# A decoder trunk's first norm: input turned unscaled and kept for the residual, the norm's factor multiplied in after the turn, the rounding split over ACT, DVE and POOL

## The reference

```python
xn = rms_norm(x, norm1_g)            # x * rsqrt(mean(x*x) + 1e-6) * g
z  = xn @ w_in + b_in                # 1024 x 7176: LRU input, q, k, v, o, gates i and f, merge gates A and B
ha = rg_lru(causal_dwconv(u), ...)   # branch A, a recurrence over positions
hb = mlstm_seq(q, k, v, i, f, ...)   # branch B, 4 heads, chunks of 64
merged = sigmoid(gA) * (ha @ w_branch_a) + sigmoid(gB) * (hb @ w_branch_b)
x = x + merged @ w_out               # the residual
x = x + ConvFFN(rms_norm(x, norm2_g))
y = rms_norm(x, final_g)
```

## Time and profile before

| | |
|---|---|
| time, median of 3 runs | 1083.74 us (1082.34 to 1083.84) |
| profiled execution | 1083.24 us, span 1081.4 us |
| PE busy | 1064.2 us, 98% |
| DVE, ACT, POOL busy | 600.7, 397.7, 367.1 us |
| DMA, mean | 101 GB/s, 109.39 MB |

### The profile page before, as it was taken

How to read it: one execution, slowest core, us unless ns; L and a number is a source line. 1 busy time by engine, 2 the same in 40 slices (tenths; PEclk the granted TensorE clock), 3 DMA queues, 4 the chain that set the end, 5 groups by cost and what they waited for, 6 DMA issues and landing times.

```text
span 1081.4 us, 19445 instructions
## 1 busy us (share of the span) xinstructions
PE 1064.2 (98%) x8029; PEld 1037.4 (96%) x8029; DVE 600.7 (56%) x946; ACT 397.7 (37%) x565; POOL 367.1 (34%) x174
## 2 busy tenths in 40 slices
PE   6999999999999999999999999999999999999997
PEld 5999999999999999899899999999999999999997
DVE  5776558845252252342543338999950189999412
ACT  6566786323433334232423343223221122222332
POOL 3343334333222222222223344433444244334330
PEclk9999999999999999999999999999999999999999
DMA  6333332236263362352462233223313222223312
GB/s 175 108 85 91 101 91 79 80 107 142 78 191 96 88 219 59 101 173 88 147 166 63 81 95 98 79 84 93 100 56 102 76 79 78 79 88 99 100 43 89
DMA packets 180689, 109.39 MB, mean 101 GB/s; under 512 B 7691, under 2 KB 176891, under 8 KB 180606
## 3 DMA queue, kind: packets, MB, share of 16 engines
q1 hardware_dynamic: 180396, 108.12, 34.7%
q10 hardware_dynamic: 210, 0.07, 0.0%
HBM read 93.56 MB, written 12.41 MB: 98 GB/s over the span
## 4 chain that ended last, share of the span: by engine, by line
PE 98%; DMA 1%; ACT 0%; DVE 0%; SPq 0%; issue 0%; DVEq 0%
PE ring L1922 48%; PE ring L2317 22%; PE bank L2317 17%; PE bank L2178 2%; PE bank L2165 1%; PE bank L1971 1%; PE bank L2148 1%; PE bank L2158 1%; PE bank L2218 1%; PE bank L2043 1%; DMA x_tok<-in_x_prompt 1%; PE bank L2206 1%; PE ring L2076 1%; PE bank L2241 0%; PE ring L1962 0%; PE bank L1950 0%
## 5 line engine op out<-in xcount | busy, mean ns | idle before, releaser
L837 POOL TENSOR_TENSOR wlo<-stage,whi 128x1024 fp32r<-128x1024 f32 x79 | 197.3, 2497 | 425.8 <-ACT whi L883 425.8
L1922 PE MATMUL ring<-xh,whi 128*128 128x282 f32 (+1 forms) x1008 | 223.7, 303 | 0.0
L1922 PE MATMUL ring<-xl,whi 128*128 128x282 f32 (+1 forms) x1008 | 218.0, 298 | 0.0
L1922 PE MATMUL ring<-xh,wlo 128*128 128x282 f32 (+1 forms) x1008 | 217.5, 297 | 0.0
L1922 PEld LDWEIGHTS ring<-xh,whi 128*128 128x128 f32 x1008 | 162.5, 188 | 8.0 <-issue 7.6
L870 POOL TENSOR_TENSOR wlo<-stage,whi 128x1024 fp32r<-128x1024 f32 (+1 forms) x40 | 109.3, 2733 | 162.9 <-ACT whi L1225 162.9
L1922 PEld LDWEIGHTS ring<-xl,whi 128*128 128x128 f32 x1008 | 163.7, 188 | 0.0
L1922 PEld LDWEIGHTS ring<-xh,wlo 128*128 128x128 f32 x1008 | 163.4, 188 | 0.0
L883 ACT ACTIVATE whi<-stage 128x1024 fp32r<-128x1024 f32 x80 | 84.3, 1054 | 87.9 <-PE ring L1922 81.4
L1225 ACT ACTIVATE whi<-stage 128x1024 fp32r<-128x1024 f32 (+1 forms) x40 | 46.0, 1154 | 100.4 <-PE ring L2317 54.0
L870 POOL TENSOR_TENSOR wlo_third<-stage,whi_third 128x1024 fp32r<-128x1024 f32 (+1 forms) x20 | 52.9, 2643 | 83.4 <-ACT whi_third L1225 83.4
(11 more groups left out here) (372 smaller groups left out, 2239.7 us busy)
## 6 DMA issues: line engine op xcount, KB each, us to landing
stage<-in_w_in SPq DMA_DIRECT2D x56, 512.0 KB, 3.8
stage<-in_w_up SPq DMA_DIRECT2D x44, 512.0 KB, 3.7
stage<-in_w_down SPq DMA_DIRECT2D x16, 704.0 KB, 4.6
stage<-in_w_branch_a SPq DMA_DIRECT2D x8, 512.0 KB, 3.9
c_sample<-in_state_mlstm_C SPq DMA_DIRECT2D x16, 256.0 KB, 5.1
out_s_mlstm_C<-c_sample SPq DMA_DIRECT2D x16, 256.0 KB, 2.4
stage<-in_w_branch_b SPq DMA_DIRECT2D x8, 512.0 KB, 4.0
stage<-in_w_out SPq DMA_DIRECT2D x8, 512.0 KB, 3.9
```

The source lines that it names most:

```text
L837: pool.tensor_tensor(wlo[:, slot, 0:n], stage[:, slot, 0:n], whi[:, slot, 0:n].bitcast(F32), ALU.subtract).then_inc(w_lo, 1)
L1922: last = pe.matmul(of(z, t0, t1), w[:, kk * P:kk * P + P], x[:, kk, t0:t1], start=kk == 0 and m == 0, stop=kk == kn - 1 and m == 2)
```

## The change

x is turned as it is loaded. ACT copies each turned job from the ring to `x_raw` (unscaled, in the place that merged takes later). The norm's factor becomes a row spread over all partitions: DVE multiplies the identity by the tile's factors (`diag`), PE multiplies a matrix of ones with it, ACT copies the result to `rrow`. DVE then multiplies ring, norm gain and rrow into one of four buffers `xn_full`, ACT rounds that to xh, POOL subtracts for xl. PE's steps wait for POOL (`xn_lo`). SP writes x_raw (2.42 MB) to a DRAM tensor `x_turned` in one DMA after the m state, ahead of weight 3, and reads it back into resid in one DMA where x_tok2 was loaded. The turns of x_tok2 and ACT's copies of them go. Tile 4's square moves to DVE, weight 1's low part from POOL to DVE, and POOL clears bd after the last difference.

```diff
@@ SP
-            load_x(x_tok, x_in)
+            for i in range(TT):
+                load_tile(x_tok, x_in, i)
...
                 sp.dma_start(mst, a["state_mlstm_m"][0].rearrange("b h -> h b")).then_inc(gate_rows_in, 16)
+
+            sp.wait_ge(raw_done, XN)
+            sp.dma_start(xdram, flat(x_raw[:, :, :])).then_inc(x_spill, 16)
...
-            load_x(x_tok2, [x2_in] * TT)
+            sp.wait_ge(hb_lo, 8)
+            sp.wait_ge(x_spill, 16)
+            sp.dma_start(flat(resid[:, :, :]), xdram).then_inc(x2_in, 16)
@@ POOL
+            def xn_low(n):
+                f, t0, t1 = job(n)
+                pool.wait_ge(xn_hi, n + 1)
+                pool.tensor_tensor(xl[:, f, t0:t1], xn_full[n % 4][:, 0:t1 - t0], xh[:, f, t0:t1].bitcast(F32),
+                                   ALU.subtract).then_inc(xn_lo, 1)
+            for n in range(4):
+                xn_low(n)
             pool.wait_ge(w_hi, 1)
             pool.tensor_tensor(gate_columns(glo), ...).then_inc(w_lo, 1)
-            lo(1, 1, D)
+            for n in range(4, XN):
+                xn_low(n)
             st.link(pool.memset(bd[0][:, :, :], 0.0))
             pool.memset(bd[1][:, :, :], 0.0).then_inc(bd_zero, 1)
+            pool.wait_ge(w_lo, 2)
             lo(2, 0, D)
@@ ACT
-            act.activation(x_tok[:, 0], x_tok[:, 0], ACT.Copy, scale=rms[:, 0:1]).then_inc(x0_scaled, 1)
...
+            def raw_copy(n):
+                act.wait_ge(tile_done, T_XN + n + 1)
+                act.activation(x_raw[:, f, t0:t1], ring_bank(n)[:, 0:t1 - t0], ACT.Copy).then_inc(raw_done, 1)
+            def row_copy(part):
+                act.wait_ge(rb_psum, part + 1)
+                act.activation(rrow[:, t0:t1], bank[:, 3 - part, 0:t1 - t0], ACT.Copy).then_inc(rb_ready, 1)
             def xn_high(n):
-                act.wait_ge(tile_done, T_XN + n + 1)
-                act.activation(xh[:, f, t0:t1], ring_bank(n)[:, 0:t1 - t0], ACT.Copy, scale=cols[...])
+                act.wait_ge(tile_evicted, T_XN + n + 1)
+                act.activation(xh[:, f, t0:t1], xn_full[n % 4][:, 0:t1 - t0], ACT.Copy).then_inc(xn_hi, 1)
...
+            for n in range(4):
+                raw_copy(n)
+            rms_of(1)
+            row_copy(0)
             square_tile(2)
             rms_of(2)
             for n in range(4):
                 xn_high(n)
+                raw_copy(n + 4)
+                if n == 1:
+                    rms_of(3)
...             (gate columns rounded)
             rms_of(4)
+            xn_high(4)
+            hi(1, 1, D, None, 16)
+            xn_high(5)
+            row_copy(1)
+            raw_copy(8)
+            raw_copy(9)
+            xn_high(6)
+            xn_high(7)
+            raw_copy(10)
+            raw_copy(11)
+            for n in range(8, 12):
                 xn_high(n)
+                raw_copy(n + 4)
+            for n in range(12, XN):
                 xn_high(n)
             hi(2, 0, D, None, loads_of(2))
...
-                    for e in range(2 if residual else 0):          # in wb_pair
-                        act.wait_ge(res_done, 2 * f - 8 + e + 1)
-                        act.activation(flat(resid[:, ds(2 * f - 8 + e, 1), :]), bank2(e)[:, 0:T], ACT.Copy)
@@ DVE
+            def rms_diag(i):
+                dve.wait_ge(rms_done, i + 1)
                 st.link(dve.reciprocal(rms[0:n, i:i + 1], rms[0:n, i:i + 1]))
-                ts(x_tok[0:n, i], x_tok[0:n, i], rms[0:n, i:i + 1], None, ALU.mult).then_inc(x_scaled, 1)
+                ts(diag[i][0:n, 0:n], ident[0:n, 0:n], rms[0:n, i:i + 1], None, ALU.mult).then_inc(diag_done, 1)
+            def xn_scaled(n):
+                dve.wait_ge(rb_ready, n // 8 + 1)
+                dve.wait_ge(raw_done, n + 1)
+                if n >= 4:
+                    dve.wait_ge(xn_lo, n - 3)
+                mul_add(xn_full[n % 4][:, 0:t1 - t0], ring_bank(n)[:, 0:t1 - t0], cols[:, C_N1 + f:C_N1 + f + 1],
+                        rrow[:, t0:t1], ALU.mult, ALU.mult).then_inc(tile_evicted, 1)
+            order: diag 0, square 1, diag 1, scaled 0-3, diag 2, squares 3 and 4, diag 3, scaled 4 5, diag 4,
+                   scaled 6 7, low part of weight 1, scaled 8-15
...
             dve.wait_ge(tile_evicted, T_OUT)
-            dve.wait_ge(res_evicted, 8)
+            dve.wait_ge(x2_in, 16)
@@ PE
-                    if i:
-                        pe.wait_ge(x_scaled, i)
-                    else:
-                        pe.wait_ge(x0_scaled, 1)
+                    pe.wait_ge(x_in[i], 32 if i in (0, TT - 1) else 16)
                     last = pe.transpose(ring_bank(n)[...], x_tok[0:m, i, P * f:P * f + P], ident[0:m, 0:m])
...
-                pe.wait_ge(tile_evicted, T_XN + 8 * part + kk + 1)     # part_step
+                pe.wait_ge(xn_lo, 8 * part + kk + 1)
...
+            def rms_rows(part):
+                for i in tiles:                                         # 0, 1 or 2, 3, 4
+                    pe.wait_ge(diag_done, i + 1)
+                    last = pe.matmul(bank[:, 3 - part, ...], ones[0:m, :], diag[i][0:m, 0:m], ...)
+                last.then_inc(rb_psum, 1)
+            rms_rows(0)
-            for n in (4, 6):
+            for n in range(4, 8):
                 next_turn(n, range(2))
-                next_turn(n + 1, range(2))
-                gate_step(0, n - 4)
-                gate_step(0, n - 3)
+            for kk in range(2):
+                gate_step(0, kk)
+            rms_rows(1)
+            for kk in range(2, 4):
+                gate_step(0, kk)
             for n in range(8, 12):
                 gate_step(0, n - 4)
                 next_turn(n, range(2, TT))
             for n in range(12, XN):
                 next_turn(n, range(2, TT))
                 gate_step(1, n - 12)
                 first_step(0, 2 * n - 24)
                 first_step(0, 2 * n - 23)
...
-                for e in range(2 if f >= 4 else 0):                     # after w_branch_b's columns
-                    n = 2 * f - 8 + e
-                    if n >= 2:
-                        pe.wait_ge(res_evicted, n - 1)
-                    token_transposes(bank2(e), n, x_tok2).then_inc(res_done, 1)
```

More of the change, by code:

```diff
@@ L285, in hybrid_layer @@
         resid = sb("resid", [P, 8, T], o_b)
+        x_raw = sb("x_raw", [P, 8, T], o_c)
+        diag = [sb(f"rms_diag{i}", [P, P], o_b + 8 * D + 512 * i) for i in range(TT)]
+        xn_full = [sb(f"xn_full{i}", [P, T - SPLIT], o_b + 8 * D + 512 * TT + 4 * (T - SPLIT) * i) for i in range(4)]
         x_tok = sb("x_tok", [P, TT, D], o_h)
+        rrow = sb("rms_row", [P, T], o_h + 4 * D * TT)
         SB = 6 * TB + 10272 + 384
+        assert 4 * D * TT + TB <= SB
         def head_slot(name, shape, off):
@@ L1192, in _, with wb_pair @@
             hi(B_WB + 1, (B_WB + 1) % 2, D, T_WB, loads_of(B_WB + 1))
-            def wb_pair(i, residual):
+            def wb_pair(i):
                 for j in range(2):
@@ L1354, in scale_tile @@
                 st.link(dve.reciprocal(rms[0:n, i:i + 1], rms[0:n, i:i + 1]))
-                ts(x_tok[0:n, i], x_tok[0:n, i], rms[0:n, i:i + 1], None, ALU.mult).then_inc(x_scaled, 1)
-            def xn_low(n):
+                ts(diag[i][0:n, 0:n], ident[0:n, 0:n], rms[0:n, i:i + 1], None, ALU.mult).then_inc(diag_done, 1)
+            def xn_scaled(n):
                 f, t0, t1 = job(n)
-                dve.wait_ge(xn_hi, n + 1)
-                mul_add(xl[:, f, t0:t1], ring_bank(n)[:, 0:t1 - t0], cols[:, C_N1 + f:C_N1 + f + 1],
-                        xh[:, f, t0:t1].bitcast(F32), ALU.mult, ALU.subtract).then_inc(tile_evicted, 1)
-            dve.wait_ge(rms_done, 1)
-            dve.reciprocal(rms[:, 0:1], rms[:, 0:1]).then_inc(x0_inv, 1)
-            square_tile(1)
-            scale_tile(1)
-            square_tile(3)
-            dve.wait_ge(tile_evicted, T_XN)
-            xn_low(0)
-            xn_low(1)
-            scale_tile(2)
-            xn_low(2)
-            xn_low(3)
-            scale_tile(3)
-            scale_tile(4)
-            for n in range(4, XN):
-                xn_low(n)
+                dve.wait_ge(rb_ready, n // 8 + 1)
[4 more added lines that the diff above has]
+                        rrow[:, t0:t1], ALU.mult, ALU.mult).then_inc(tile_evicted, 1)
+            dve.wait_ge(const_done, 2)
+            rms_diag(0)
+            square_tile(1, 0)
+            rms_diag(1)
+            dve.wait_ge(tile_evicted, T_XN)
+            for n in range(4):
+                xn_scaled(n)
+            rms_diag(2)
+            square_tile(3, 1)
+            square_tile(4, 2)
+            rms_diag(3)
+            xn_scaled(4)
+            xn_scaled(5)
+            rms_diag(4)
+            xn_scaled(6)
+            xn_scaled(7)
+            dve.wait_ge(w_hi, 2)
+            dve.wait_ge(w_lo, 1)
+            tt(wlo[:, 1, 0:D], stage[:, 1, 0:D], whi[:, 1, 0:D].bitcast(F32), ALU.subtract).then_inc(w_lo, 1)
+            for n in range(8, XN):
+                xn_scaled(n)
```

(15 more changed lines are left out.)

61 lines of the change are left out of this document (23 added, 38 removed).

## The result

The changed kernel takes 1100.37 us, median of 6 runs (1099.88 to 1103.05), against 1083.22 (1082.34 to 1083.84) for the kernel before: a ratio of 1.0165, 95% interval 1.0152 to 1.0178. The profiled execution is the slowest of the six: 1103.05 us with a span of 1101.3, against 1083.24 and 1081.4 before. PE is busy 1067.0 us (before 1064.2) and 97% of the span. It does forty transposes less and ten short matmuls more (the norm row's), so nearly all of the 20 us are waits and a slower pace.

What follows compares the result with a forecast made beforehand. The prediction took PE's queue plus its few gaps as the bound: 1083.24 (profiled) - 4.08 (second turn) + 18.5 (late product 2, front's 7 included) + 1.6 (clock) = 1099.2 us. Own range 1095 to 1105, with rivals 1090 to 1108.

Steps and rivals of the forecast that it cites:

- Second turn, -4.08: Branch-b stage: removing PE's four groups of x_tok2 turns, 1.02 us each, saves 4.08 us; nothing else comes late there.
- The loop, 1.8 us a job: Front, second part: turn, raw copy, rounding, difference and gate step wait in a circle, 1.8 us a job against 1.46.
- rival B: Front and spill: the loop never forms and the spill holds nothing, product 2 at 41.2, total 1080.6 us; chance 0.05.
- Product 1 at 40.3: End of the front: PE's product 1 starts at 40.3 us instead of 33.24, so the front alone is +7 us.
- the walk: Front: four queues stepped through in written order with estimated durations, PE changing to its faster pace at 18.5 us.
- rival C: Front: gaps keep PE at its 1.2 GHz level, product 2 at 66.0, total 1107 us; chance 0.10.
- bd's clearing and SP's queue: Behind the front: POOL's clearing ends at 37.9, SP reaches the spill at 43.2 and issues weight 3 at 43.6 us.
- The spill, weight 3 landing 11.4 us behind its issue: SP's queue: 2.42 MB ahead of weight 3 delay its landing to 54.6 us; product 2 starts at 58.3 instead of 39.8.
- Rival A: SP's queue: the spill does not hold weight 3, product 2 at 51.1, half the clock's charge, total 1091.3 us; chance 0.13.
- The clock, +1.6: PE after its 11 us gap before product 2: 3.3 us at half pace cost 1.6 us, bounds 0 to 1.7.
- Sum: Whole kernel: 1083.24 - 4.08 + 18.5 + 1.6 = 1099.2 us, the 18.5 containing the front's 7; forecast's chance 0.70.

Runs made afterwards that it cites:

- e4: Kernel before without the second turn: PE's forty transposes and ACT's copies out, resid loaded from w_up, residual not computed; 1079.64 us, ratio 0.9970.
- e7: e4 with ACT's wait for m_lo moved behind the rounding of w_out's second weight, residual not computed; 1078.28 us, ratio 0.9958 to the kernel before.
- e8: e6 with ACT's wait for m_lo moved behind the rounding of w_out's second weight, nothing left out; 1082.85 us, ratio 1.0000 to the kernel before.
- e5: e2 with turns 8 to 11 and 12 to 15 ahead of each part's gate steps in PE's queue; 1084.13 us, ratio 1.0011 to the kernel before.
- e1: Changed kernel with the spill cut to 32 bytes a partition, resid loaded from w_up, residual not computed; 1095.73 us, ratio 1.0118 to the kernel before.
- e2: Changed kernel with POOL clearing bd before the sixteen differences instead of after them; 1088.74 us, ratio 1.0057 to the kernel before.
- e3: Changed kernel with bd cleared first and the spill cut to 32 bytes a partition, residual not computed; 1089.41 us, ratio 1.0058 to the kernel before.
- e6: e5 with the gate columns rounded and subtracted behind job 1 instead of job 3; 1084.15 us, ratio 1.0011 to the kernel before.
- b4: Kernel before without second turn: xh and xl spilled, read back and summed by DVE, branch-b weights but the last rounded one step ahead; 1083.10 us, ratio 0.9998.
- b5: b4 with weights rounded ahead in the last branch-b column and w_out too, and DVE's sums begun earlier; 1083.06 us, ratio 1.0000 to the kernel before.

## Why the prediction was right

The forecast was 1099.2 us and the time is 1100.37; the mechanism is the one forecast. That it came within 1.2 us is partly luck. All three quantities that its own range rests on fell outside their bounds: bd was clear at 42.2 (36 to 40), the landing took 10.0 (10.9 to 14.9), the clock cost 2.43 (0 to 1.7). By its own steps, against the profiled execution:

- *Second turn, -4.08.* The four stretches are gone and nobody waits for the residual's readback. Mis-sized: "nothing else comes late there" looked only at the branch-b columns. w_out's second weight came 0.93 us late in the changed kernel as in e4; e7 and e8 name the cause. The turns themselves are worth 4.33 (e7's chain), so the net is 3.4.
- *The loop, 1.8 us a job.* Right, 3.6 for two jobs, and e5, which takes it apart, gains 4.6 us. The waits in it add to 4.2. With the loop rival B is out.
- *Product 1 at 40.3.* Mis-sized: 44.60. In e1's execution it is 42.87, so 1.7 us belong to the profiled run's late input (its first tile landed at 6.5, 1.4 us later than in the trace of before). The gate columns were ready at 19.2 instead of 16.0, which PE waited 4.7 us for; 1.2 of these 3.2 us are the late input too (18.04 in e1). From there to product 1 it took 25.3 us instead of 24.3, and here the walk had the pace wrong: it let PE change to the faster one at 18.5, but the nine products of 1.92 us above are still 0.21 us apart, and the change lies near 24.9 (22.4 in e1, 21.6 in e2, 23.6 in e5). So rival C was true of the first part of the front. Whether the waits or the turns put the change off is not shown.
- *POOL and DVE in that walk.* It had no entry for their holding each other up. Beside POOL's differences DVE's 0.29-us diagonal took 0.76 and its square 1.76 instead of 1.22 (ACT's root of tile 3 waits for that square, and the gate columns' rounding stands behind it), and one 256-column difference of POOL's took 2.04 instead of the usual 0.7, beside DVE's low part of weight 1. DVE's timeline of the changed kernel, before POOL's first difference and in it:

```profile
10.43 0.29 DVE L1393 TENSOR_SCALAR rms_diag<-ident,misc 128x128 f32<-128x128 f32 x1
...
13.84 0.76 DVE L1393 TENSOR_SCALAR rms_diag<-ident,misc 128x128 f32<-128x128 f32 x1
```

```profile
13.80 1.41 POOL L857 TENSOR_TENSOR xl<-xn_full,xh 128x256 fp32r<-128x256 f32 x2 [6.47 <-ACT xh L966]
```

- *bd's clearing and SP's queue.* The step that carries the result, shown by e2. Forecast: cleared at 37.9, spill issued at 43.2; measured 42.2 and 47.49, late by the front's error alone: POOL's last difference ended at 40.2 instead of 36.0. The 5.3 us of SP's issues held.
- *The spill, weight 3 landing 11.4 us behind its issue.* It took 10.0, nearer to the 10.9 that y's rows gave. Rival A is out: the weight, issued 0.4 us after the spill, needed 9.6 us where 4.0 is usual, and e1 gets 5 us of it back.
- *The clock, +1.6.* Mis-sized: 2.43 (8.99 against 6.56), above its upper bound of 1.7. The charge came from the 3.3 us at the start; the trace after has about 5 us below full clock. Rival C as a whole is out: turns and steps in the second part go at full pace.
- *Sum.* Product 2 is 21.25 us later (forecast 18.5), 2.43 for the clock, 0.93 for w_out's second weight, less 4.33 for the turns: 20.3 us. By the chain PE comes to the stage behind w_out 20.5 us later (666.80, before 646.28). The span is 19.9 us longer; the other 0.6 lie behind PE's last products, where y is written out. The median is 2.7 us below the profiled execution, and its late input accounts for 1.7. So the forecast's nearness to the median owes something to errors that cancel: a front put too short, the clock too cheap and w_out's wait at nothing, against a landing too late and an input that usually comes earlier.

What each part cost, from medians: bd's clearing behind the differences 11.6 us with the spill there (e2), of which the spill takes part only while the clearing is late (4.6, e1; nothing, e3); turns interleaved with steps that wait for POOL 4.6 (e5); the rest of the longer front and the uncovered wait what the turns give (e8), that rest being by its rows mostly PE's slower pace until 24 us.

## What to carry to other kernels

Follow each queue past the point of a moved operation: two clearings of 1 us, put behind sixteen differences, held five microseconds of DMA issues, a 2.4 MB spill and the weight that PE needed, and cost 11.6 us. Work that is removed may be the cover of a wait elsewhere, so look for the latest arrival in the stages behind it too, and price a gap of some microseconds on PE at its length and about 1.5 to 3 us more. Waits taken away early in this program gained less than their length, since the change to the faster pace moved as well: e6 waited 1.7 us less than e5 and gained nothing. An engine's idle time is not free for new work when another engine must share its way to memory.

## What the runs showed of the hardware

**DVE and POOL.** In b4, from 546 to 600 us, eight DVE operations with all their operands in SBUF started while POOL subtracted a weight; each ended 0.61 to 0.63 us after POOL's did (562.20 + 2.12 = 564.32 against 560.91 + 2.78 = 563.69; 580.83 + 2.31 = 583.14 against 580.11 + 2.41 = 582.52), which is about what it takes alone. An operation that reads PSUM and SBUF (sig_gb<-ring) in the same stretch stayed at 0.75. That fits a DVE that does not run slower but stands still until POOL is through; and POOL's 2.4 us became 2.6 to 2.8 where it began behind such an operation of DVE. An operation with one tensor in SBUF and a factor per partition was held up too: the diagonal above (0.76 for 0.29), and in the kernel before the convolution's first tap at 41.89, 2.45 us beside POOL's subtraction of 41.04 to 44.00, where it takes 0.59 when POOL is still. The Trainium skill (SBUF — State Buffer, Who interferes with whom) says that a DVE operation with both inputs in SBUF and a GpSimd operation that reads SBUF contend for a shared pair of ports, and that this is an exclusive lock: whoever is issued first has it and the other is blocked. The trace agrees, by the 0.62 us above. It was not in the prediction, where it would have lengthened the front.

**Short gaps and the clock.** 1.95 us of waiting in b4 and 2.43 in b5, after hundreds of microseconds at full clock, were each followed by 3 to 4 us at matmul pairs 0.48 us apart instead of 0.27 (granted clock 0.77 from 605 to 610 us in b4 and 0.76 from 598 to 605 in b5), 1.5 us lost. The waits of 4.6 and 9.6 us (e1, changed kernel) cost 2.9 and 2.4. After the 0.9-us wait of e4 no fall shows: the granted clock is 1.00 from 597 to 605 us.
